# First feed-forward of the third part in three parts, fourteen of its 22 column tiles by seven quarter products; the wave tables made inside the first two layers

## The reference

```python
for l in range(2):                                   # the first two layers
    x = hybrid_layer(x, ...)                         # mixer, then:
    #   f = jnp.square(jax.nn.relu(h @ w_up)) @ w_down      (1024 -> 4096 -> 1024)
# the third part
def swiglu_ffn(x, w_in, w_down):                     # 1024 -> 2 * 2816 -> 1024
    a, b = jnp.split(x @ w_in, 2, axis=-1)
    return (jax.nn.silu(a) * b) @ w_down

x = x + 0.5 * swiglu_ffn(rmsnorm(x, ffn1_norm), ffn1_w_in, ffn1_w_down)   # "ffn1"
...                                                  # S5 scan, dilated attention, memory attention
x = x + 0.5 * swiglu_ffn(rmsnorm(x, ffn2_norm), ffn2_w_in, ffn2_w_down)   # "ffn2"
```

## Time and profile before

| | before |
|---|---|
| three runs | 2402.18 / 2402.59 / 2402.71 us |
| the profiled execution | 2402.1 us, its span 2400.3 us |
| TensorE's mean granted clock | 0.999 of full |
| PE busy | 2385.4 us, 99% of the span, 13482 matmuls |
| DVE busy | 1591.3 us, 66% |
| ACT busy | 1094.6 us, 46% |
| POOL busy | 344.6 us, 14% |
| DMA | 260.13 MB, mean 108 GB/s |
| the chain that ended last | PE 91%, DVE 5%, ACT 2%, issue 2% |

### The profile page before, as it was taken

The page is one execution under the profiler, slowest core; times in us unless marked ns, Lnnn a source line. Parts: engine busy times, 40 slices in busy tenths (PEclk is TensorE's granted clock), DMA queues, the critical chain, the costliest instruction groups (busy, mean ns, idle before and its releaser), DMA issues.

```text
span 2400.3 us, 33986 instructions
## 1 busy us (share of the span) xinstructions
PE 2385.4 (99%) x13482; PEld 2014.5 (84%) x13482; DVE 1591.3 (66%) x2231; ACT 1094.6 (46%) x1626; POOL 344.6 (14%) x259
## 2 busy tenths in 40 slices
PE   9999999999999999999999999999999999999998
PEld 7877998998886989889988888877778788889997
DVE  7775775665977567557644347769995386359685
ACT  5346553555445546336522236522335564335444
POOL 1231030001132121001111124300000121120001
PEclk9999999999999999999999999999999999999999
DMA  4312222323230222223232225643442143222322
GB/s 169 145 45 88 89 87 90 123 88 106 101 128 18 106 90 104 88 106 109 86 105 89 103 102 183 221 148 119 145 158 80 49 169 134 88 106 82 114 87 88
DMA packets 46849, 260.13 MB, mean 108 GB/s; under 512 B 5424, under 2 KB 7984, under 8 KB 22768
## 3 DMA queue, kind: packets, MB, share of 16 engines
q1 hardware_dynamic: 44448, 249.07, 29.6%
q0 software_dynamic: 640, 5.51, 0.6%
q10 hardware_dynamic: 1616, 3.54, 0.5%
HBM read 240.27 MB, written 16.78 MB: 107 GB/s over the span
## 4 chain that ended last, share of the span: by engine, by line
PE 91%; DVE 5%; ACT 2%; issue 2%; DMA 0%; DVEq 0%; SPq 0%; ACTq 0%
PE gemm L487 60%; PE gemm L1104 5%; PE gemm L1105 5%; PE gemm L1106 5%; PE gemm L780 1%; PE gemm L791 1%; PE gemm L782 1%; DVE w_lo L437 1%; DVE out_sb L1912 1%; PE turned L1418 1%; PE mixed L1432 1%; PE score L1409 1%; PE gemm L520 1%; PE gemm L673 1%; PE gemm L674 1%
## 5 line engine op out<-in xcount | busy, mean ns | idle before, releaser
L437 DVE TENSOR_TENSOR w_lo<-w_raw,w_hi 128x2048 fp32r<-128x2048 f32 (+4 forms) x157 | 341.9, 2177 | 204.9 <-ACT w_hi L429 204.8
L487 PE MATMUL gemm<-h_hi,w_hi 128*128 128x512 f32 x1136 | 454.2, 400 | 1.0 <-DVE w_lo L437 1.0
L487 PE MATMUL gemm<-h_hi,w_lo 128*128 128x512 f32 x1136 | 443.3, 390 | 0.0
L487 PE MATMUL gemm<-h_lo,w_hi 128*128 128x512 f32 x1136 | 442.7, 390 | 0.0
L429 ACT ACTIVATE w_hi<-w_raw 128x2048 fp32r<-128x2048 f32 (+4 forms) x167 | 292.9, 1754 | 202.9 <-PE gemm L487 169.0
L487 PEld LDWEIGHTS gemm<-h_hi,w_hi 128*128 128x128 f32 x1136 | 213.6, 188 | 55.5 <-issue 8.3
L487 PEld LDWEIGHTS gemm<-h_hi,w_lo 128*128 128x128 f32 x1136 | 213.2, 188 | 45.5
L487 PEld LDWEIGHTS gemm<-h_lo,w_hi 128*128 128x128 f32 x1136 | 213.6, 188 | 42.2 <-issue 1.0
L487 PE MATMUL gemm<-f_hi,w_hi 128*128 128x512 f32 x480 | 187.2, 390 | 0.7
L487 PE MATMUL gemm<-f_hi,w_lo 128*128 128x512 f32 x480 | 186.8, 389 | 0.0
L487 PE MATMUL gemm<-f_lo,w_hi 128*128 128x512 f32 x480 | 186.8, 389 | 0.0
(11 more groups left out here) (549 smaller groups left out, 5315.9 us busy)
## 6 DMA issues: line engine op xcount, KB each, us to landing
w_raw<-in_w SPq DMA_DIRECT2D x179, 1024.0 KB, 4.8
w_raw<-in_w SPq DMA_DIRECT2D x12, 768.0 KB, 4.2
w_raw<-in_w SPq DMA_DIRECT2D x17, 512.0 KB, 3.8
trig_kept<-made SPq DMA_DIRECT2D x16, 512.0 KB, 5.9
trig<-trig_kept SPq DMA_DIRECT2D x16, 512.0 KB, 6.5
w_raw<-in_w SPq DMA_DIRECT2D x8, 640.0 KB, 4.5
bias_t<-in_att_bias SPq DMA_DIRECT2D x2, 1536.0 KB, 9.1
decay_t<-in_c_decay SPq DMA_DIRECT2D x2, 1536.0 KB, 8.0
```

Source lines behind the costliest of these rows:

```text
L437: dve.tensor_tensor(flat(w_lo, b), flat(w_raw, b), flat(w_hi, b).bitcast(F32), ALU.subtract).then_inc(S["w_rest"], 1)
L487: mm = pe.matmul(dst, lhs, rhs, start=b.first and k == 0 and j == 0, stop=b.last and k == b.kt - 1 and j == 2)
```

## The change

Three things change together.

1. ffn1 is built like ffn2: parts of 8, 8, 6 tiles, 14 of the 22 up blocks by seven quarter products, a down projection behind each part, its result added to `x_sb` three times instead of once. The functions of ffn2 (`seven_part`, `down_rests`, `down_rounds`, `up_gated`, ...) now take a name and serve both. The sums for its seven blocks, `last_sum` included, are all DVE's.
2. The waves leave ffn1. They are made in the down blocks of parts 1 and 2 of both layers: one wave for each of 4 down blocks, 2 parts and 2 layers (`wave_at`). The small preparing steps are made in part 0 of the first layer (DVE, `steps_and_turns`) and in its first down block of part 1 (ACT, `step_angles`). The scratch `made` now has one buffer, and ACT itself issues the store.
3. The memory's norm moves to the second part of ffn1, and the squares of tiles 4 and 5 of x now come on ACT behind the last down block's rounding, together with those of 6 and 7.

```diff
 for part in range(1, PARTS):                                   # POOL, in a layer
-    for b in plan1[UP[part]:UP[part] + 4]:
+    for b in plan1[UP[part] + (part > 1):UP[part] + 4]:
         last_sum(pool, b)
+    if part == 1:
+        pool.wait_ge(S["units"], plan1[DOWN[1]].u0)
+        pool.dma_start(time_t[:], A["c_time"]).then_inc(S["time_in"], 16)
+        pool.wait_ge(S["time_in"], 16 * (lay + 1))
+        pool.wait_ge(S["coef_r"], 1)
+    if part < PARTS - 1:
+        for j in range(4):
+            whole_turns(pool, wave_at(lay, part, j))
+            if j == 2:
+                last_sum(pool, plan1[UP[part + 1]])
...
                         for q in range(2) if j == 2 else range(2, 4):   # ACT, down block j
                             pair_round(act, begun, q)
+                    if part:
+                        waves(act, wave_at(lay, part, j))
+                        if j == 3:
+                            log_and_exp(act)
...
                         for q in range(2, 4):                           # DVE, down block j
                             pair_rest(dve, begun, q)
+                    if part:
+                        phases(dve, wave_at(lay, part, j))
...
+        def whole_turns(pool, s):
+            if s:
+                pool.wait_ge(*wave_stored(s - 1))
+            to = made[:, 0, :]
+            pool.tensor_scalar(to, time_t[:], sp_[:, 9, s:s + 1], MAGIC, ALU.mult,
+                               ALU.add).then_inc(S["turns_a"], 1)
+            pool.wait_ge(S["turns_a"], s + 1)
+            pool.tensor_scalar(to, to, MAGIC, None, ALU.subtract).then_inc(S["turns_s"], 1)
...
+        def waves(act, s):
+            act.wait_ge(S["phased"], s + 1)
+            cos, sin = made[:, 0, :], made[:, 1, :]
+            act.activation(cos, sin, ACT.Abs).then_inc(S["trig_s"], 1)
+            act.wait_ge(S["trig_s"], 3 * s + 1)
+            act.activation(sin, sin, ACT.Sin, scale=BELOW_2PI).then_inc(S["trig_s"], 1)
+            act.activation(cos, cos, ACT.Sin, scale=-BELOW_2PI, bias=quarter[:, 0:1]).then_inc(S["trig_s"], 1)
+            act.wait_ge(S["trig_s"], 3 * s + 3)
+            act.dma_start(trig_kept[s], made[:]).then_inc(S[f"trig_moved{s % 3}"], 16)
...
+        def phases(dve, s):
+            to = made[:, 1, :]
+            dve.wait_ge(S["turns_s"], s + 1)
...
-FFN_PARTS = (6, 6, 5, 5)
...
-    ffn("ffn1")
+    gated("ffn1")
```

More of the change, by code:

```diff
@@ L254, in third_pieces @@
         out.append(Piece(0, c, WCOLS, KD, "feat", "w_out2"))
[L255 to L267, removed]
+    gated("ffn2")
     return out, start
@@ new lines, in third_tensor, with mem_total @@
+            opening_in_halves(pe, ups[:2], 2 * DEPTH - 1, sq_f)
+            for n, b in enumerate(ups[2:]):
+                product(pe, b, h_hi, h_lo, each=None if n else second_total(pe, 2 * DEPTH - 1, sq_f))
+            for part in range(len(GATED_PARTS)):
+                if part:
+                    seven_part("ffn1", part)
+                ups, downs = gated_blocks("ffn1", part)
+                for j, b in enumerate(downs):
+                    def mem_total(m):
+                        if (part, j, m) == (1, 1, 1):
+                            pe.wait_ge(S["sq_added"], added_by(MEM_NORM))
+                            pe.matmul(o_ps[:, 0:MEM], ones[:], mem_sq[:, 0, :], start=True,
+                                      stop=True).then_inc(S["norm_sum"], 1)
+                    product(pe, b, g2_hi, g2_lo, tile_ready=None if j else (S["g2_s"], sum(GATED_PARTS[:part])),
+                            halfway=mem_total)
@@ new lines, in down_rounds @@
+            def down_rounds(name, part, j):
+                ups, downs = gated_blocks(name, part)
+                if part == 0 and j == 0:
+                    direct_round(act, gated_counts(name), ups[-1])
+                if part == 0 and j == 2:
+                    sums_round(act, gated_counts(name))
+                if j < 2 or part == LAST_PART:
+                    round_block(act, downs[j].n + 2)
+                else:
+                    begun = gated_blocks(name, part + 1)[0][0]
+                    for q in range(2) if j == 2 else range(2, 4):
+                        pair_round(act, begun, q)
@@ L2945, in third_scalar @@
+            norm_squares(act, x_sb, x2_sq, wait=(S["g_free"], downs[0].t0), tiles=(KD - 2, KD - 1))
             norm_rooted(act, N0 + 2)
@@ L3223, in third_scalar @@
[L3223 to L3237 removed]
+                    seven_part("ffn2", part)
@@ L3238, in third_scalar @@
+                if part < LAST_PART:
+                    for j, b in enumerate(downs):
+                        down_rounds("ffn2", part, j)
             log_and_exp(act)
```

712 lines of the change are left out of this document (311 added, 401 removed).

## The result

The changed kernel takes 2434.83 us (median of four runs, 2433.88 to 2435.28); beside it the kernel before took 2402.39 us (2402.05 to 2402.71). The ratio is 1.0134, 95% interval 1.0121 to 1.0148: slower by 32.4 us. The forecast was 2417.1 us with a range of 2405 to 2431. The direction and the place were right, the size lies outside the range.

A forecast was written before the change was run, and what follows sets the result against it. TensorE was taken as the bound, by number and kind of matmuls while no other engine is late. 2402.1 - 11.2 (ffn1's up blocks) + 23.2 (four layer boundaries) + 3.0 (end of ffn1) = 2417.1 us; range 2405 to 2431.

The forecast's parts named there:

- ffn1's blocks: ffn1's up part: 14 plain blocks of 10.88 us become seven-product blocks of 10.08 us, 11.2 us less.
- The mechanism at the boundary: After layers' down parts 1 and 2, fourth wave and table load delay `two_sum`: 5.8 us a boundary, 23.2 us in all.
- The store: Wave's store in the boundary chain, with no load under way: taken as 2.65 us, the unknown of that term.
- The price of the turns: GpSimd's turns in the wave chain at the boundary: 2.31 us from their start to the phases' start.
- The delay goes no further: First seven block behind a boundary: 1.3 us more at `three_sum`, next block's halves ready before PE ends the block.
- The end of ffn1: Squares of tiles 4 and 5 come later, so PE waits 2.6 to 4.2 us longer for VectorE's add; 3.0 us taken.
- the lower clock behind the halt: Behind a TensorE halt: a lowered clock would make the prediction wrong; no profile row priced it.
- D: Rival: table load drains ACT, its own 1.28 us once more at each boundary, 2422.2 us; chance 0.05.
- B: Rival: ACT's stores take the median 5.9 us, each boundary 3.25 us more, 2430.1 us; chance 0.16.
- C: Rival: part hides, a boundary costs 0.85 to 3.25 us, 2397.8 to 2407.4 us, no change told; chance 0.07.
- A: Rival: nothing waits at the boundaries, only first and last terms stand, 2393.9 us, faster; chance 0.10.
- both waiting terms: The layers' four boundaries, 23.2 us in all, and the end of ffn1, 3.0 us, both added time.

The follow-up runs named there:

- e1: Changed kernel with each wave's VectorE phases and ScalarE sines, and the table load, ahead of the layers' down-block adds and rounds; 2410.6 us, ratio 1.0034.
- e7: Changed kernel with VectorE's phases ahead of the adds, ScalarE's fourth wave and table load behind `two_sum`, ffn1's end in its old order; 2392.26 us, ratio 0.9957.
- e8: Changed kernel with, on ScalarE alone, the fourth wave, its store and the table load moved behind the copy to `two_sum`; 2422.29 us.
- e9: Changed kernel with `last_sum` of down block j = 2 made by VectorE behind its other sums, not by GpSimd; 2431.39 us.
- e10: Changed kernel with a separate buffer for the whole turns, so VectorE's phases wait for the store and GpSimd does not; 2422.75 us.
- e2: Changed kernel with 50 unused matmuls ahead of TensorE's wait in the four boundary blocks; 2435.62 us.
- e4: Changed kernel with ScalarE's and VectorE's orders at the end of ffn1 put back as before the change; 2428.36 us.
- e6: Changed kernel without the call that loads the logarithm and exponential table behind each part's fourth wave; 2436.2 us.
- e3: Changed kernel with the waves ahead of the down blocks' adds and rounds, except each part's fourth, which stays behind its block; 2422.69 us.
- e11: e7 with parts of 6, 8, 8 tiles in ffn1 and ffn2, so more tiles go by seven products; 2407.14 us.

## Why the prediction missed

**ffn1's blocks.** Right: 11.2 us expected, 10.6 us measured.

**The mechanism at the boundary.** Right in kind and place: e1 and e7 remove the wait by order alone, e8, e9 and e10 each take away one link. The step that failed is the size of this term, 5.8 us a boundary and 23.2 us in all, where 36.5 us were lost. Its first part, the wait, was put at 4.5 us, and the gaps are 5.88 and three times 6.88 us: 8.5 us of the 13.3 missed. The timelines of GpSimd and VectorE in the changed kernel, ahead of the first boundary:

```profile
406.38 1.88 POOL L2338 TENSOR_SCALAR made<-made 128x512 f32<-128x512 f32 x1
406.82 1.10 DVE L1013 TENSOR_TENSOR w_sums<-w_raw 128x512 f32<-128x512 f32 x1
```

Against the steps in the prediction, at the first boundary: the third wave's phases began at 412.2, not 411.6, for the most part because this weight sum took 1.10 us beside the turns of the third wave, not 0.69 as before. The turns of the fourth took 2.86 us, not 2.31: their first step took 1.25 us beside a subtraction on VectorE (418.80), not 0.70. Both are read from rows that overlap and not tested. The store took 2.68 us, as priced. At the other three boundaries, which the forecast took to be like the first, the 1.0 us of the stretched halves comes on top (shown by e9).

The price of the turns came from a row where VectorE was idle; the trace of before also has the same step at 1.23 us (1476.33), beside a VectorE subtraction. The Trainium skill, "SBUF — State Buffer", section "SBUF: two separate sides", says that GpSimd and a VectorE operation with two SBUF inputs shut each other out of a shared port pair for a whole instruction. The rows in the second layer agree with that: there the two engines end one behind the other, 1.1 us apart, which would be so if each had waited for the other in turn.

**"The delay goes no further."** Wrong, and the second part of the same term: the other 5 us. The forecast had 1.3 us behind the wait; each boundary loses 2 to 3 us there. Without any low clock (e2) it is 1.0 to 1.6 us at `three_sum` in the first seven block and 0.3 to 0.4 us each in the second and, at the first boundary, in the fourth; with the low clock it is about the same. The sums on VectorE catch up only over several blocks. Per boundary 6.6 us of mean gap and some 2.5 us behind it make the 9.1 us that 36.5 / 4 gives, where 5.8 was expected.

**The end of ffn1.** 3.0 us expected, 6.7 measured. The forecast had a wait of 2.6 to 4.2 us longer and took 3.0, near GpSimd's shorter time; 4.4 came, with GpSimd's two adds at 4.26 us. The 2.3 us beyond are put down to the lower clock behind the halt, which the prediction named as unpriced. e4 gives the whole back, 6.5 us.

**The rivals.** A table load that drains ScalarE (D) is ruled out by e6: three of the waits shrink by 1.3 to 1.4 us, the load's own length, and the fourth by that and the unstretched halves. The rule of the Trainium skill, "ScalarE: Activation LUTs", section "What ACT_TABLE_LOAD costs", some 1.38 us of drain beside the load, is not what this case shows. Slow stores (B) did not come: the median of the 16 is 2.6 us. A part that hides (C) did not come either; its bounds, by the prediction's own terms, are 2397.3 and 2406.9 us, not 2397.8 and 2407.4. That nothing waits (A) is what e7 reaches, but only by another order, and with the end of ffn1 put back too: 2392.26 us, where the prediction's terms without both waits give 2390.9.

**The sum.** Layers 36.5 instead of 23.2, end 6.7 instead of 3.0, ffn1's blocks 0.6 short: 17.6 us, against the 17.7 between 2417.1 and 2434.8. The direction is no luck: every term has the right sign and place, and both waiting terms were too small.

What stays open: how the 36.5 us divide exactly between gap, clock and `three_sum`, since the last two overlap, and why the clock fell behind three of e3's four equal halts and not behind the second. That VectorE's token sums set e11's halt was read from its timeline and not tested.

## What to carry to other kernels

A side job laid into another engine's slack is placed by order, not by amount: before moving it, write down what stands behind it in the same queue at the place where the bounding engine next waits. Here the same work cost the layers 36.5 us or about 1 us (e7), by its places in two queues, and moving the fourth wave on one engine alone gave back a third of it (e8).

When a chain crosses VectorE and GpSimd, price its steps from rows where both work at once, if the trace has them, and look for a second late sum behind the first wait before writing that a delay ends there.

A low clock behind a halt cost next to nothing where TensorE would have waited for another engine at full speed (e2, e3). Before pricing it, ask what it would wait for then.

## What the hardware showed

Behind gaps of 5.88 and 6.88 us TensorE's clock was at 1.2 GHz instead of 2.4 for about 3.8 to 6.0 us. Behind four gaps of 3.55 us in e3 it was lower for 2.9, 3.4 and 5.8 us and once not at all; behind one of 2.92 us in e8 it was lower too, behind one of 1.76 us in e1 it stayed at 1.00. Matmuls without use kept it at 1.00 through the same wait. Beside each other, a GpSimd sum went from 1.30 to 2.23 us and a VectorE subtraction from 1.21 to 2.31, the rows ending in turn. A 512 KB store issued by ScalarE landed in 2.6 us (median of 16).
